# First taps of ten convolution tiles moved to ScalarE and GpSimd, and tile 13 divided between TensorE and VectorE

## The reference, cut to what matters

```python
proj = h @ w_in + b_in
val, glu_gate, z = jnp.split(proj, 3, axis=-1)
u = val * jax.nn.sigmoid(glu_gate)
u = lax.conv_general_dilated(
    u, conv_w[:, None, :], window_strides=(1,), padding=[(CONV_KERNEL - 1, 0)],
    dimension_numbers=('NWC', 'WIO', 'NWC'), feature_group_count=CONV_WIDTH) + conv_b
u = jax.nn.silu(layer_norm(u, norm_g, norm_b))
u = u * jax.nn.silu(z)
return u @ w_out + b_out
```

## Time and profile before

| | before |
|---|---|
| median of 3 runs | 806.0 us |
| profiled execution | 809.28 us, of which the span is 807.5 us |
| PE busy | 793.3 us (98% of the span) |
| DVE busy | 590.0 us (73%) |
| POOL busy | 521.3 us (65%) |
| ACT busy | 374.3 us (46%) |
| input projection and convolution, up to the mean | about the first 277 us |

### The profile page before, as it was taken

The page is one execution under the profiler, slowest core; times in us unless marked ns, Lnnn a source line. Parts: engine busy times, 40 slices in busy tenths (PEclk is TensorE's granted clock), DMA queues, the critical chain, the costliest instruction groups (busy, mean ns, idle before and its releaser), DMA issues.

```text
span 807.5 us, 11221 instructions
## 1 busy us (share of the span) xinstructions
PE 793.3 (98%) x3835; PEld 671.2 (83%) x3835; DVE 590.0 (73%) x1003; ACT 374.3 (46%) x660; POOL 521.3 (65%) x318
## 2 busy tenths in 40 slices
PE   7999999999999999999999999999999999999996
PEld 6888888888888888888998788888898889888885
DVE  2499999999999869993723290048789888876217
ACT  4433544535353478621432444156767666655110
POOL 4567989989797773684455357337777676377430
PEclk9999999999999999999999999999999999999999
DMA  5445555655574414643233326226666755663412
GB/s 198 130 132 134 159 164 153 185 149 157 157 185 117 144 53 139 201 130 105 79 113 109 105 78 170 65 56 194 189 199 193 213 181 152 188 188 128 157 52 105
DMA packets 132367, 115.14 MB, mean 143 GB/s; under 512 B 17530, under 2 KB 109792, under 8 KB 132316
## 3 DMA queue, kind: packets, MB, share of 16 engines
q1 hardware_dynamic: 132316, 114.49, 48.3%
HBM read 91.01 MB, written 14.80 MB: 131 GB/s over the span
## 4 chain that ended last, share of the span: by engine, by line
PE 95%; DMA 2%; DVE 1%; ACT 0%; issue 0%; SPq 0%; DVEq 0%
PE bank L1806 88%; DMA x_in<-in_x_dram 1%; PE bank L1894 1%; PE bank L2117 1%; PE bank L1891 1%; PE bank L2118 1%; PE bank L1892 1%; DMA prob_moved<-prob_kept 1%; DMA prob_kept<-prob 0%; PE bank L1991 0%; PE bank L2110 0%; DVE prob L1703 0%; PE bank L1824 0%; PE bank L2044 0%; PE bank L2108 0%
## 5 line engine op out<-in xcount | busy, mean ns | idle before, releaser
L805 POOL TENSOR_TENSOR w_lo<-w_raw,w_hi 128x1024 fp32r<-128x1024 f32 x102 | 253.6, 2496 | 123.5 <-ACT w_hi L998 116.4
L1426 DVE SCALAR_TENSOR_TENSOR bank<-u,conv_w,bank 128x512 f32<-128x512 f32 x301 | 199.9, 748 | 0.0
L998 ACT ACTIVATE w_hi<-w_raw 128x1024 fp32r<-128x1024 f32 x102 | 107.3, 1057 | 114.3 <-DMA w_raw<-in_a_w_in_dram 50.6
L1806 PE MATMUL bank<-xt_hi,w_lo 128*128 128x512 f32 (+1 forms) x392 | 152.5, 389 | 0.0
L1806 PE MATMUL bank<-xt_lo,w_hi 128*128 128x512 f32 (+1 forms) x392 | 151.1, 385 | 0.0
L1806 PE MATMUL bank<-xt_hi,w_hi 128*128 128x512 f32 (+1 forms) x392 | 151.0, 385 | 0.0
L1806 PEld LDWEIGHTS bank<-xt_lo,w_hi 128*128 128x128 f32 x392 | 73.9, 189 | 15.2 <-issue 0.5
L1806 PEld LDWEIGHTS bank<-xt_hi,w_lo 128*128 128x128 f32 x392 | 73.9, 189 | 15.0 <-issue 0.5
L1806 PEld LDWEIGHTS bank<-xt_hi,w_hi 128*128 128x128 f32 x392 | 73.9, 188 | 14.9
L1806 PE MATMUL bank<-ht_hi,w_lo 128*128 128x512 f32 (+1 forms) x208 | 76.4, 367 | 0.0
L1806 PE MATMUL bank<-ht_lo,w_hi 128*128 128x512 f32 (+1 forms) x208 | 75.8, 365 | 0.0
(11 more groups left out here) (220 smaller groups left out, 1725.6 us busy)
## 6 DMA issues: line engine op xcount, KB each, us to landing
w_raw<-in_a_w_in_dram SPq DMA_DIRECT2D x48, 512.0 KB, 3.9
w_raw<-in_b_w_in_dram SPq DMA_DIRECT2D x20, 512.0 KB, 3.6
prob_kept<-prob SPq DMA_DIRECT2D x16, 640.0 KB, 3.3
prob_moved<-prob_kept SPq DMA_DIRECT2D x64, 160.0 KB, 3.2
stacked<-u_kept SPq DMA_DIRECT2D x64, 132.0 KB, 4.1
w_raw<-in_a_w_out_dram SPq DMA_DIRECT2D x16, 512.0 KB, 4.0
w_raw<-in_b_w_out_dram SPq DMA_DIRECT2D x16, 512.0 KB, 3.6
bundle_raw<-in_b_w_uq_dram SPq DMA_DIRECT2D x16, 256.0 KB, 4.2
```

The costliest lines, as they stand in the source:

```text
L805: nc.gpsimd.tensor_tensor(w_lo[slot][:], w_raw[raw][:], w_hi[slot][:].bitcast(F32), ALU.subtract).then_inc(w_lo_ready, 1)
L998: nc.scalar.activation(w_hi[slot][:], w_raw[raw][:], ACT.Copy).then_inc(w_hi_ready, 1)
L1426: nc.vector.scalar_tensor_tensor(out=inner[:] if k < TAPS - 1 else acc[:, t, :], in0=u[:, t, k:k + SEQ], scalar=conv_w[:, column:column + ...
L1806: last = nc.tensor.matmul(out_ap, a, b, start=(start and n == 0 and m == 0), stop=(stop and n == len(parts) - 1 and m == 2))
```

## The change

`PREFIX` names ten VectorE tiles and a number of taps. Of each, ACT and POOL do the first taps (52 in all), as they did for tiles 3 and 14 before; VectorE takes their sum from `acc` as the start of its first running sum. ACT also makes the first product of the second running sum (`start_second`, one instruction per tile, into a tile of `z_a`, or for tiles 14 and 15 into a finished tile of `u`). `start_second` waits until VectorE has finished the tile two places before in the list, whose buffer it reuses. Tile 3 becomes a VectorE tile, and so does tile 13 for its taps 0 to 14; TensorE keeps taps 15 to 30 of tile 13, which halves its matmuls there. `add_parts` takes bias and first part in one instruction. The low part of the matrix tiles' input has a buffer of its own in `z_a`, for which a wait is added in the z stage. In a pair, the first products now stand ahead of the gate (`BEFORE_GATING`).

```diff
-        LATE_TILE, LATE_TAPS = 14, 9
-        SHARED_TILES = (3,)
-        PAIR_SHARE = {5: 2, 6: 4, 7: 3, 8: 4, 9: 1, 10: 4, 11: 3, 12: 4, 13: 1, 14: 4, 15: 3}
-        Z_SHARE = {0: 1, 1: 2, 4: 2, 5: 2}
+        PREFIX = {3: 5, 4: 8, 6: 5, 7: 3, 8: 7, 10: 5, 11: 4, 12: 6, 14: 4, 15: 5}
+        HALF_TILE, HALF_END = MATRIX_TILES[-1], REACH - 1
+        VECTOR_TILES = tuple(t for t in range(CT) if t not in MATRIX_TILES[:-1])
+        shared_taps = [(t, k) for t, taps in PREFIX.items() for k in range(taps)]
+        PAIR_SHARE = {5: 5, 6: 5, 7: 3, 8: 5, 9: 3, 10: 5, 11: 2, 12: 5, 13: 3, 14: 5, 15: 2}
+        Z_SHARE = {0: 2, 1: 2, 4: 3, 5: 2}
+        BEFORE_GATING = 3
...
-        POOL_SUM = SHARED_TILES + (0, 2, 4, 6) + MATRIX_TILES[:3] + (7, 8, 10, 11, 12)
-        PARTS_AFTER = {7: 0, 11: 1, 12: 2, LATE_TILE: 3}
+        POOL_SUM = (0, 2, 3, 4, 6, 7, 8, 10, 11) + MATRIX_TILES[:3] + (12,)
+        PARTS_AFTER = {6: 0, 10: 1, 14: 2, 15: 3}
...
+        def chains(t):
+
+            first, middle = PREFIX.get(t, 0), middle_tap(t)
+            return (first, middle), (middle + 1 if t in PREFIX else middle, last_tap(t))
+
+        def second_start(t):
+
+            n = list(PREFIX).index(t)
+            return z_a[:, n % 2, :] if t < 14 else u[:, t - 7, PAD:]
...
+            def start_second(t):
+
+                before = [of for of in PREFIX if of < t]
+                if len(before) > 1:
+                    act.wait_ge(tap_done, whole_at()[before[-2]])
+                k = middle_tap(t)
+                nc.scalar.activation(second_start(t), u[:, t, k:k + SEQ], ACT.Copy,
+                                     scale=conv_w[:, t * TAPS + k:t * TAPS + k + 1]).then_inc(second_ready, 1)
...
+                elif k == first and t in PREFIX:
+                    if first < middle_tap(t):
+                        dve.wait_ge(product_added, prefix_added(t))
+                    else:
+                        dve.wait_ge(second_ready, STARTED.index(t) + 1)
+                    nc.vector.scalar_tensor_tensor(out=inner[:], in0=moved, scalar=tap,
+                                                   in1=acc[:, t, :] if first < middle_tap(t) else second_start(t),
+                                                   op0=ALU.mult, op1=ALU.add).then_inc(tap_done, 1)
...
-                nc.vector.tensor_scalar(inner[:], acc[:, t, :], vec[:, V_CONVB + t:V_CONVB + t + 1], None, ALU.add
+                if t == HALF_TILE:
+                    nc.vector.tensor_tensor(inner[:], unmoved_part(m), moved, ALU.add).then_inc(tap_done, 1)
+                else:
+                    nc.vector.scalar_tensor_tensor(out=inner[:], in0=unmoved_part(m), scalar=vec[:, V_CONVB + t:V_CONVB + t + 1],
+                                                   in1=moved, op0=ALU.add, op1=ALU.add).then_inc(tap_done, 1)
...
-                windows = [slice(REACH * s, REACH * s + SEQ) for s in range(STEPS)]
-                for s, window in enumerate(windows):
-                    nc.tensor.matmul(out[:], matrix_lo[:, g, s, :], stacked[:, 0, g, window], start=s == 0, stop=False)
+                steps = kept_steps(m)
+                for s in steps:
+                    window = slice(REACH * s, REACH * s + SEQ)
+                    nc.tensor.matmul(out[:], matrix_lo[:, g, s, :], stacked[:, 0, g, window], start=s == steps[0], stop=False)
```

More of the change, by code:

```diff
@@ L484, in middle_tap, with last_tap @@
+        def last_tap(t):
+            return HALF_END if t == HALF_TILE else TAPS
         def middle_tap(t):
[L486 to L498, removed]
+            first = PREFIX.get(t, 0)
+            return first + (last_tap(t) - first + 1) // 2
@@ L511, in whole_at, with adds_of, kept_steps @@
-            return ends
+            for t in VECTOR_TILES:
+                done += sum(end - first for first, end in chains(t)) + 1
+                ends[t] = done
+                if t in PARTS_AFTER:
+                    done += adds_of(PARTS_AFTER[t])
+                    ends[MATRIX_TILES[PARTS_AFTER[t]]] = done
+            return ends
+        def adds_of(m):
+            return PARTS if MATRIX_TILES[m] == HALF_TILE else PARTS - 1
+        def kept_steps(m):
+            return range(STEPS - 1, STEPS) if MATRIX_TILES[m] == HALF_TILE else range(STEPS)
@@ L513, in pair_taps, with unmoved_part @@
+        def unmoved_part(m):
+            return u[:, 3, PAD:] if MATRIX_TILES[m] == HALF_TILE else acc[:, MATRIX_TILES[m], :]
         def pair_taps(t):
@@ L829, in value_gate @@
                     conv_input_lo(BEGINS.index(t))
[L830 to L833, removed]
+                for low in range(2):
+                    if t in ((4, 5)[low], BEGINS[1] + 2, BEGINS[2] + 2):
+                        pack_matrices((t - 4) // 4, low)
+                for n in pair_taps(t)[BEFORE_GATING:]:
                     add_product(n)
@@ L1439, in add_parts @@
                 t, inner = MATRIX_TILES[m], bank[CONV_BANK[0]]
+                first, second, third = PART_TILES[m % 2]
                 for i in range(2):
@@ L1450, in add_parts @@
-                shift = PART_SHIFT * (PARTS - 1)
-                dve.wait_ge(tap_done, done + PARTS - 1)
-                nc.vector.tensor_tensor(acc[:, t, :], u[:, PART_TILES[m % 2][0], PAD - shift:PAD - shift + SEQ], inner[:],
-                                        ALU.add).then_inc(tap_done, 1)
+                shift = 3 * PART_SHIFT
+                moved = u[:, first, PAD - shift:PAD - shift + SEQ]
+                if t == HALF_TILE:
[3 more added lines that the diff above has]
+                                                   in1=moved, op0=ALU.add, op1=ALU.add).then_inc(tap_done, 1)
@@ new lines, in add_parts @@
+                shift = PART_SHIFT
+                dve.wait_ge(tap_done, done + 1)
+                nc.vector.tensor_tensor(inner[:, shift:], u[:, third, PAD:PAD + SEQ - shift], inner[:, shift:], ALU.add
+                                        ).then_inc(tap_done, 1)
+                shift = 2 * PART_SHIFT
+                dve.wait_ge(tap_done, done + 2)
+                nc.vector.tensor_tensor(inner[:] if t == HALF_TILE else acc[:, t, :],
+                                        u[:, second, PAD - shift:PAD - shift + SEQ], inner[:], ALU.add).then_inc(tap_done, 1)
@@ L1455, in convolve @@
+                if t == HALF_TILE:
+                    dve.wait_ge(tap_done, done + 3)
+                    nc.vector.tensor_tensor(acc[:, t, :], acc[:, t, :], inner[:], ALU.add).then_inc(tap_done, 1)
             def convolve():
                 done = 0
-                for group in vector_groups():
+                for t in VECTOR_TILES:
                     last_of = [done, done]
+                    wait(dve, tap_done, done)
                     for n in range(TAPS):
-                        for slot, (t, first, end) in enumerate(group):
+                        for slot, (first, end) in enumerate(chains(t)):
```

77 lines of the change are left out of this document (31 added, 46 removed).

## The result

The changed kernel takes 823.62 us (823.24 to 826.05), the kernel before 806.24 us on the same chip (805.62 to 806.77): a ratio of 1.0222 (95% interval 1.0201 to 1.0243), slower. The forecast was 824.1 us. Its first tap starts at 28.14 us, 3.62 us earlier than that of before: its start was quicker, with 1.2 us as TensorE's longest wait for the input instead of 3.8. Times of the two pages are compared with that shift.

A forecast was written before the change was run, and what follows sets the result against it. PE's matmul list was taken to set the time, VectorE at most 0.4 us ahead at the mean. VectorE's -2.9, +17.4 and +1.9 delay the mean 16.4 us; clock adds 1.7: 824.1 us from 806.0, range 803.8 to 835.

The forecast's parts named there:

- The sum: VectorE up to the mean: count, openings and prefix wait together start the mean 16.4 us later; with clock, +18.1 us.
- Openings, +17.4: On VectorE, 20 of 24 instructions with two SBUF inputs wait for POOL, 0.87 us each: 17.4 us.
- rival 1: VectorE's openings with two SBUF inputs pay nothing: 805.0 us, or 803.2 with the prefix in time; chance 0.28.
- The four counted as free: Part sums of tiles 1 and 5 and tile 10's two openings cost nothing extra, POOL being empty then.
- The forecast's own lower bound: Lower end of the forecast's own range, about 814 us, at 0.45 us instead of 0.87 per opening.
- Count, -2.9: VectorE's instructions up to the mean: taps -4.6, joined tiles +3.8, part additions -2.1, sum -2.9 us.
- The prefix wait, 1.9: VectorE, after tile 2, waits 1.9 us for POOL's prefix of tile 3; later prefixes are ready before it.
- TensorE, -2.8: Tile 13's four packs lose 12 matmuls, so TensorE is ready for the mean 2.8 us earlier, at 274.3 us.
- Clock, +1.7: After TensorE's idle gap before the mean, a lowered granted clock loses 1.7 us, added once.
- ACT's hold: At tile 8, ACT's second start waits 7 us for VectorE, likewise tiles 11 and 12; PE's stalls stay hidden.
- 8 us or so: Sign that the forecast is right: PE waits about this long at the mean for VectorE's channel sum.
- rival 2: ACT's holds at tiles 8, 11 and 12 starve PE beyond the hidden 19.2 us: some 835 to 842 us; chance 0.10.

The follow-up runs named there:

- run 1: Changed kernel with all 24 openings reading the PSUM bank instead of a second SBUF input, every wait kept, sums incomplete: 807.34 us, ratio 1.0004 to the kernel before.
- run 2: Changed kernel with only the ten second openings reading the PSUM bank instead of the second start, which is left out of the sum: 815.92 us, ratio 1.0113.
- run 6: Kernel before, with nine tiles' second-chain openings given a second SBUF input, same instruction count and waits: 817.96 us, ratio 1.0147.
- run 3: Changed kernel with four places for the second starts, so ScalarE waits for the fourth tile before instead of the second: 830.74 us, ratio 1.0306.
- run 8: Changed kernel without second starts, VectorE doing those ten taps itself, prefixes still read as second input of first openings; full computation: 827.08 us, ratio 1.0258.
- run 4: Changed kernel with both all openings reading the PSUM bank and four places for the second starts: 808.03 us, ratio 1.0028 to the kernel before.
- run 5: Kernel before with only tile 13's 12 matmuls taken off TensorE, that half of its taps left out of the sum: 807.61 us, ratio 1.0014.

## Why the prediction was right

**The sum.** Forecast for VectorE up to the mean: -2.9 by count, +17.4 for the openings, +1.9 for the prefix, together +16.4 us. From its first tap to the end of the channel sum VectorE took 276.66 - 31.76 = 244.9 us before and 288.86 - 28.14 = 260.7 us after: +15.8 us. From the first tap to the end of the span it is 807.5 - 31.76 = 775.7 and 821.4 - 28.14 = 793.3 us, +17.5 us, where the forecast's sum had +18.1.

**Openings, +17.4.** Measured 17.3 for the 20 openings of L1447, and 0.7 for the part sums (3.0 us for three of L1475, against 2.3 in run 1): 18.0 us. The mechanism is the one forecast: the ends lie 0.55 us behind GpSimd's, as in the earlier trace rows, also where the result goes to PSUM. That it is the second input, and not lateness, runs 1, 2 and 6 show. Run 1, without those inputs, is the forecast's rival 1 acted out. In the changed kernel itself rival 1 fell: 17.3 / 20 is 0.87 us per opening, where it needed less than 0.05. The rule of the Trainium skill (SBUF — State Buffer, Who interferes with whom) held here, by run 6's 1.80 us against 0.75 for the same instruction count and the same waits, and by the ends behind GpSimd's.

**That the size was hit is in part luck.** The 0.87 us was the mean of another line at another stage, and two errors cancelled: 17 of the 24 were held up and not 20, for 18.0 / 17 = 1.06 us each and not 0.87. The runs show that the price is no property of the instruction: the mean excess was 0.84 us (run 2), 1.05 (run 6), 1.18 (run 3) and 1.34 (run 8), and the two highest are of kernels without the hold. The four counted as free were free, and ScalarE's hold, the reason given, ends each time just before GpSimd's gap does (133.05, 173.09 and 190.42 us). The two of tile 12 fell into another gap, in which GpSimd and ScalarE waited for TensorE's gate; whether that is an echo of the earlier holds is not shown. Run 3 shows what the holds were worth: without them, 7 us more. The forecast's own lower bound is a slip: by its sum 0.45 us per opening gives 824.1 - 20 x 0.42 = 815.7 and not 814; nothing hangs on it.

**Count, -2.9.** Mis-sized: it was about -4.6. The changed kernel gives 15.8 - 18.0 - 2.4 = -4.6. Run 1 gives the same: 273.09 - 27.49 = 245.6 us from first tap to channel sum, less 5.3 us of prefix waits, is 240.3, against 244.9 before. The timelines tell which part. Seven taps fewer, -4.6, and three part additions fewer, -2.1, came as counted. What the tiles take beside their taps (opening, end and join, with a tap at 0.66 us) grew from 9.3 to 11.4 us, +2.1 and not +3.8. The forecast took 0.94 us for each joined tile from the kernel before, where the next instruction starts 0.85 us after an opening:

```profile
32.61 0.75 DVE L1422 TENSOR_SCALAR bank<-u,conv_w 128x512 f32<-128x512 f32 x1
```

That opening starts at 31.76 us. In the changed kernel it is 0.73 us (28.14 to 28.87), and 0.67 after a prefixed opening in a gap of GpSimd (173.09 to 173.76).

**The prefix wait, 1.9.** Measured 2.38 us, at tile 3 and nowhere else, as forecast. Run 1 shows the condition that the prediction named, "as it is late": with VectorE in time, tile 4's prefix is late as well, by 2.9 us.

**TensorE, -2.8.** Right, and worth nothing. Without holds, run 3 has it ready at 294.2 - 23.6 = 270.6 us and run 4 at 273.6 + 0.15 - 2.9 = 270.8 us, where 277.1 - 2.8 - 3.62 = 270.7 was forecast. The sentence that a gain on TensorE alone ends at the meeting 0.4 us away is run 5's result; that the leftover gap costs more clock than the 0.4 us gains it had not said.

**Clock, +1.7.** From the start of the mean's product to the end of the span it was 530.4 us before (807.5 - 277.1) and 821.4 - 289.0 = 532.4 us after: +2.0 us.

**ACT's hold.** The forecast had three holds of 7 us and a few us lost on TensorE, hidden. ScalarE's waits of this kind sum to 19.6 us, five of them; the three at tiles 8, 11 and 12 took 7.7, 4.9 and 5.3. TensorE stood idle for 8.4 us and ran at half clock behind each gap, so that it was ready for the mean at 289.0 - 4.8 = 284.2 us and not at 270.7: 13.5 us lost, all hidden. The wait at the mean was therefore 4.8 us and not "8 us or so": rival 2 came nearer than the text made it, though run 3 shows that it was not what set the time. One of the signs named was wrong outright: TensorE's busy time did not fall by 2.8 us but rose by 4.3, mostly because of matmuls at half clock.

## What to carry to other kernels

Before work is handed to another engine, look at where the inputs of the instruction that takes it back will lie: here an opening with a second start took 17.9 / 10 = 1.79 us, some 1.0 more than a tap, and saved one tap of 0.66; an opening with a prefix cost 0.7 us more (1.3 in run 8) and saved three to eight. When two engines meet within half a microsecond at a join, relieving one of them can gain no more than that, and the gap it leaves can cost clock: run 5 took 12 matmuls away and gained none of them. And a stall elsewhere may be what keeps a shared resource free: price the removal of a hold by what the freed engine will then do.

## What was not expected of the hardware

Removing ScalarE's hold made the kernel 7 us slower (run 3), and it did so through the second inputs: with all openings from the bank the same edit cost 0.7 us (run 4 against run 1). That two instructions with two SBUF inputs back to back do not pass together the forecast had read from the earlier trace rows; new is what comes between them, GpSimd's next instruction (97.24 us above), for the whole of which the second opening waits. And a gap of 2.2 us on TensorE at the mean was followed by a granted clock of 0.50 for two microseconds and 0.67 for two more (run 5, 274 to 278 us): 1.7 us of clock, more than the 0.4 us that the relief could gain.
